# Two-block transformer layer stack: attention scores as pairs of 64-row products, with the gating term in a pass of its own

## The reference

```
for l in range(2):
    h = rms_norm(x, attn_pre_g[l]);  proj = h @ w_in[l]          # 512 x 3080
    qa, ka, va, qb, kb, vb, f_logit = split(proj)                # five 512-wide parts, vb, and 8 forget columns
    # "diff" heads: 4 heads, each with two maps m of 64 features, rotary on qa and ka
    p[m] = softmax(causal(qa[h, m] @ ka[h, m].T / 8))            # m = 0, 1
    oa   = (p[0] - lam * p[1]) @ va[h]                           # va[h] is 128 wide, then rms_norm
    # "fox" heads: 8 heads of 64 features, with a forget gate
    log_f = log_sigmoid(f_logit + forget_bias[l]);  c = cumsum(log_f over tokens)
    ob   = softmax(causal(qb[h] @ kb[h].T / 8 + c[q] - c[k])) @ vb[h]
    x = x + rms_norm(concat(oa, ob) @ w_out[l], attn_post_g[l])
    x = x + rms_norm((silu(h2 @ w_gate[l]) * (h2 @ w_up[l])) @ w_down[l], ffn_post_g[l])
# then the second block: stick-breaking attention, HGRN2 mixer, feed-forward (untouched)
```

## Time and profile before

| | us |
|---|---|
| time, median of 3 runs | 2193.34 |
| profiled execution: time | 2193.14 |
| profiled execution: span | 2191.3 |
| TensorE (PE) busy | 2127.4 |
| VectorE (DVE) busy | 785.8 |
| ScalarE (ACT) busy | 749.4 |
| GpSimd (POOL) busy | 849.6 |

### The profile page before, as it was taken

How to read it: one execution, slowest core, us unless ns; L and a number is a source line. 1 busy time by engine, 2 the same in 40 slices (tenths; PEclk the granted TensorE clock), 3 DMA queues, 4 the chain that set the end, 5 groups by cost and what they waited for, 6 DMA issues and landing times.

```text
span 2191.3 us, 27815 instructions
## 1 busy us (share of the span) xinstructions
PE 2127.4 (97%) x10510; PEld 1759.3 (80%) x10510; DVE 785.8 (36%) x1513; ACT 749.4 (34%) x1287; POOL 849.6 (39%) x390
## 2 busy tenths in 40 slices
PE   8999999999999999999999999998899999999999
PEld 6886798888887876798888887776777789888887
DVE  6327542121004128452111014587566543121200
ACT  4236452222224136452222124444432434222211
POOL 3530134444434430134444434333444344444442
PEclk9999999999999999999999999999999999999999
DMA  5330033333323320033333222211211232333232
GB/s 186 106 96 1 1 92 114 99 98 97 97 87 105 97 77 1 11 97 106 96 96 96 97 86 68 77 49 40 61 45 49 83 110 84 99 96 96 87 101 72
DMA packets 130832, 178.25 MB, mean 81 GB/s; under 512 B 11891, under 2 KB 79790, under 8 KB 130734
## 3 DMA queue, kind: packets, MB, share of 16 engines
q1 hardware_dynamic: 130142, 175.25, 26.2%
q10 hardware_dynamic: 592, 1.64, 0.2%
HBM read 174.76 MB, written 2.10 MB: 81 GB/s over the span
## 4 chain that ended last, share of the span: by engine, by line
PE 39%; issue 32%; POOL 17%; DVE 9%; ACT 3%; POOLq 0%; DMA 0%; ACTq 0%; DVEq 0%
POOL w_lo L571 17%; PE PS L1504 9%; PE PS L1506 9%; PE PS L1505 9%; PE PS L1773 3%; PE PS L1785 2%; PE PS L1906 1%; DVE R L1413 1%; PE PS L1761 1%; DVE R2R L1350 1%; PE PS L1712 1%; DVE R L1421 1%; PE PS L1881 1%; PE PS L1558 1%; PE PS L1873 0%
## 5 line engine op out<-in xcount | busy, mean ns | idle before, releaser
L571 POOL TENSOR_TENSOR w_lo<-R,w_hi 128x1024 fp32r<-128x1024 f32 (+1 forms) x288 | 680.0, 2366 | 950.9 <-ACT w_hi L653 892.5
L653 ACT ACTIVATE w_hi<-R 128x1024 fp32r<-128x1024 f32 (+1 forms) x288 | 299.2, 1042 | 954.0 <-PE PS L1506 953.4
L1504 PE MATMUL PS<-xt_hi,w_hi 128*128 128x512 f32 (+1 forms) x1216 | 458.8, 377 | 0.0
L1506 PE MATMUL PS<-xt_hi,w_lo 128*128 128x512 f32 (+1 forms) x1216 | 453.2, 373 | 0.0
L1505 PE MATMUL PS<-xt_lo,w_hi 128*128 128x512 f32 (+1 forms) x1216 | 453.0, 373 | 0.0
L1504 PE MATMUL PS<-w_hi,xt_hi 128*128 128x512 f32 x928 | 375.5, 405 | 13.1 <-DVE R L1314 6.9
L1506 PE MATMUL PS<-w_hi,xt_lo 128*128 128x512 f32 x928 | 364.2, 392 | 0.0
L1505 PE MATMUL PS<-w_lo,xt_hi 128*128 128x512 f32 x928 | 363.5, 392 | 0.0
L1506 PEld LDWEIGHTS PS<-xt_hi,w_lo 128*128 128x128 f32 x1216 | 229.1, 188 | 40.6
L1505 PEld LDWEIGHTS PS<-xt_lo,w_hi 128*128 128x128 f32 x1216 | 229.3, 189 | 40.4 <-issue 1.0
L1504 PEld LDWEIGHTS PS<-xt_hi,w_hi 128*128 128x128 f32 x1216 | 229.2, 189 | 40.4 <-issue 1.0
(11 more groups left out here) (252 smaller groups left out, 2146.8 us busy)
## 6 DMA issues: line engine op xcount, KB each, us to landing
R<-in_w_in SPq DMA_DIRECT2D x56, 512.0 KB, 3.7
R<-in_w_gate SPq DMA_DIRECT2D x88, 256.0 KB, 2.8
R<-in_w_up SPq DMA_DIRECT2D x88, 256.0 KB, 3.0
R<-in_w_down SPq DMA_DIRECT2D x40, 512.0 KB, 3.8
raw<-in_w_in SPq DMA_DIRECT2D x36, 512.0 KB, 3.7
R<-in_w_out SPq DMA_DIRECT2D x24, 512.0 KB, 3.8
R<-in_w_ffn_gate SPq DMA_DIRECT2D x44, 256.0 KB, 2.8
R<-in_w_ffn_up SPq DMA_DIRECT2D x44, 256.0 KB, 3.0
```

The source lines that it names most:

```text
L571: nc.gpsimd.tensor_tensor(w_lo[:, r, 0:subs, :], raw_of(stage, lap)[:, r, 0:subs, :], w_hi[:, r, 0:subs, :].bitcast(F32), ALU.subtract).th ...
L653: nc.scalar.activation(w_hi[:, r, 0:subs, :], raw_of(stage, lap)[:, r, 0:subs, :], ACT.Copy).then_inc(hi_ready, 1)
L1504: mm(out_, a_hi, b_hi, start=start, stop=False)
L1506: return mm(out_, a_lo, b_hi, start=False, stop=stop)
```

## The change

A pair of units (two maps of a diff head, or two fox heads side by side) is now issued together, at even u. Its two score products have 64 rows each: the first uses partitions 0 to 63 of q and k, the second 64 to 127, and they write two neighbouring banks. The diff q is copied out once, without the zeros. Fox heads are transposed two at a time as full 128-row items, so there are 16 items instead of 24.

The gate is no longer in q and k. Minus c, split into a rounded part and a remainder, is placed by DVE in a tile `decay`, four TensorE transposes (at unit `COLUMNS_AT` = 2) and one ACT copy turn it into `decayT`, and a fox score pair gets a second pair of 64-row products in fp32r with `pair_rows` (0/1 rows that pick the head) over all its columns. Adding c of the query is dropped, since the softmax does not see it. `pair_rows` and the zeroing of `decay` are made by DVE during the projection, after chunk 2.

DVE takes one maximum for the two banks of a pair. The chain that makes c runs beside the transposes, and TensorE computes the sums after the last item. `PRODUCT` goes from 6 to 7 and `OUTPUT` from 7 to 8.

```diff
-JOIN, TURN, PRODUCT, OUTPUT = 2, 5, 6, 7
+JOIN, TURN, PRODUCT, OUTPUT = 2, 5, 7, 8
+COLUMNS_AT, SUMS_BANK, COLUMNS_BANK = 2, 6, 7
...
-            items1 += [(QA[:, :, cols], P, [q[:, h, :] for q in QAT], one_head[:, 0, :]), (KA[:, :, cols], P, KAT[:, h, :], 1.0)]
-        for h in range(8):
-            items1 += [(QB[:, :, h, :], 66, QBT[0:66, h, :], HD ** -0.5), (KB[:, :, h, :], 66, KBT[0:66, h, :], 1.0)]
+            items1 += [(QA[:, :, cols], P, QAT[:, h, :], HD ** -0.5), (KA[:, :, cols], P, KAT[:, h, :], 1.0)]
+        for h in range(4):
+            cols = slice(h * P, (h + 1) * P)
+            items1 += [(QB[:, :, cols], P, QBT[:, h, :], HD ** -0.5), (KB[:, :, cols], P, KBT[:, h, :], 1.0)]
...
-        units1 += [("fox", (h, 0), i) for h in range(8) for i in range(T)]
+        units1 += [("fox", (2 * pair + m, m), i) for pair in range(4) for i in range(T) for m in range(2)]
...
+                        if u == COLUMNS_AT:
+                            act.wait_ge(c_turned, l + 1)
+                            nc.scalar.activation(decayT, PS[:, COLUMNS_BANK, :], ACT.Copy).then_inc(c_copied, 1)
...
+                dve.wait_ge(c_mm, l + 1)
+                c_sum = PS[:, SUMS_BANK, 0:T * 8].rearrange("p (t a m) -> p t a m", a=4, m=2)
+                parts = [decay_r[:, :, HD * m:HD * m + 8].rearrange("p t (a b) -> p t a b", b=2) for m in range(2)]
+                for m in range(2):
+                    ins = V.tensor_scalar(parts[m][:, :, :, 0], c_sum[:, :, :, m], -1.0, None, ALU.mult)
+                link(ins)
+                for m in range(2):
+                    ins = V.scalar_tensor_tensor(parts[m][:, :, :, 1], c_sum[:, :, :, m], -1.0,
+                                                 parts[m][:, :, :, 0].bitcast(F32), ALU.mult, ALU.subtract)
+                ins.then_inc(c_placed, 1)
...
-                        V.tensor_reduce(nmax[:, u % 4:u % 4 + 1], PS[:, u % 4, 0:P * (i + 1)], AX.X, ALU.max,
-                                        negate=True).then_inc(max_done, 1)
+                    if u < len(units1) and u % 2 == 0:
+                        i, bank = units1[u][2], u % 4
+                        dve.wait_ge(s_mm, b + u + 2)
+                        V.tensor_reduce(nmax[:, bank:bank + 2], PS[:, bank:bank + 2, 0:P * (i + 1)], AX.X, ALU.max,
+                                        negate=True).then_inc(max_done, 2)
...
                         if b + u >= 4:
-                            pe.wait_ge(exp_done, b + u - 3)
-                        mm(PS[:, u % 4, 0:upto], q, kk, start=True, stop=False)
-
-                        mm(PS[:, u % 4, upto - P:upto], ident_b[:, :], causal_b[:, :], start=False, stop=True).then_inc(s_mm, 1)
+                            pe.wait_ge(exp_done, b + u - 2)
+                        if kind == "fox":
+                            pe.wait_ge(c_copied, l + 1)
+                        for m in range(2):
+                            mm(PS[:, u % 4 + m, 0:upto], q[halves[m], pair, upto - P:upto], kk[halves[m], pair, 0:upto],
+                               start=True, stop=False)
+                        if kind == "fox":
+                            for m in range(2):
+                                mm(PS[:, u % 4 + m, 0:upto], pair_rows[halves[m], pair, :], decayT[halves[m], 0:upto],
+                                   start=False, stop=False)
+                        for m in range(2):
+                            mm(PS[:, u % 4 + m, upto - P:upto], ident_b[:, :], causal_b[:, :], start=False,
+                               stop=True).then_inc(s_mm, 1)
+                    if u == COLUMNS_AT:
+                        pe.wait_ge(c_placed, l + 1)
+                        for t in range(T):
+                            last = nc.tensor.transpose(PS[:, COLUMNS_BANK, t * P:(t + 1) * P], decay[:, t, :], ident[:, :])
+                        last.then_inc(c_turned, 1)
```

More of the change, by code:

```diff
@@ L260, in build @@
         rot = at2(16560, 4, T, ROT * 8)
-        QBT = at1(0, 8, SEQ)
-        KBT = at1(4096, 8, SEQ)
+        QBT = at1(0, 4, SEQ)
+        KBT = at1(2048, 4, SEQ)
+        decay = at2(18608, T, P)
+        decay_r = at2r(18608, T, P)
+        decayT = at2r(17584, 1, SEQ)[:, 0, :]
+        pair_rows = at2r(18096, 4, P)
         YG_out = at2(4096, T, D).rearrange("p t (k n) -> p t k n", n=P)
@@ L1155, in attention1 @@
                     src = banks(c % 2)
[L1156 to L1163, removed]
+                    if c == 5:
+                        V.tensor_copy(VB[:, :, :, 0:HD], heads(src, 8)).then_inc(evac[1], 1)
+                    elif c >= 2:
+                        V.tensor_copy(dst[c], src).then_inc(evac[c % 2], 1)
+                        if c == 2:
+                            V.memset(VB[:, :, :, HD:HD + 1], 1.0)
+                            V.memset(decay, 0.0)
+                            for n in range(4):
+                                own = ident[:, :].rearrange("p (m r) -> p m r", m=2)[:, :, 2 * n:2 * n + 2]
+                                ins = V.tensor_reduce(rsum[:, n:n + 1], own, AX.XY, ALU.add)
+                            link(ins)
+                            for n in range(4):
+                                ins = V.tensor_scalar(pair_rows[:, n, :], SUMS[:, ONES, :], rsum[:, n:n + 1], None, ALU.mult)
+                            ins.then_inc(pair_rows_done, 1)
                     else:
@@ L1734, in attention1 @@
                     transpose_item(n, base, items1, 2 + n % 6, 6)
-                pe.wait_ge(f_gate, l + 1)
-                mm(PS[:, 0, 0:8 * T], SUMS[:, UPTO, :], fy[:, 2, :, :], start=True, stop=False)
-                for back in range(1, T):
-                    last = mm(PS[:, 0, 8 * back:8 * T], SUMS[:, ONES, :], fy[:, 2, 0:T - back, :],
-                              start=False, stop=back == T - 1)
-                last.then_inc(c_mm, 1)
-                pe.wait_ge(c_placed, l + 1)
                 for n in range(8, len(items1)):
@@ L1746, in attention1 @@
                 pe.wait_ge(tr_dve, (base + len(items1)) // 2)
+                pe.wait_ge(f_gate, l + 1)
+                sums = PS[:, SUMS_BANK, :]
+                mm(sums[:, 0:8 * T], SUMS[:, UPTO, :], fy[:, 2, :, :], start=True, stop=False)
+                for back in range(1, T):
+                    last = mm(sums[:, 8 * back:8 * T], SUMS[:, ONES, :], fy[:, 2, 0:T - back, :],
+                              start=False, stop=back == T - 1)
+                last.then_inc(c_mm, 1)
                 b, bo, bj = len(units1) * l, n_out * l, n_join * l
@@ L1763, in attention1 @@
                         last.then_inc(pt_mm, 1)
[L1764 to L1775 removed]
+                    if u < len(units1) and u % 2 == 0:
+                        kind, (h, _), i = units1[u]
+                        upto = P * (i + 1)
+                        pair, q, kk = (h, QAT, KAT) if kind == "diff" else (h // 2, QBT, KBT)
+                        halves = slice(0, HD), slice(HD, P)
+                        if b + u >= 4:
+                            pe.wait_ge(exp_done, b + u - 2)
+                        if u == 0:
+                            pe.wait_ge(pair_rows_done, l + 1)
+                        if kind == "fox":
[10 more added lines that the diff above has]
+                               stop=True).then_inc(s_mm, 1)
```

59 lines of the change are left out of this document (25 added, 34 removed).

## The result

The changed kernel takes 2174.59 us (median of 4 runs, 2172.83 to 2175.07), the kernel before on the same chip 2193.32 us (2190.09 to 2193.53). The ratio is 0.9917 with an interval of 0.9899 to 0.9934: faster, by 0.8%. The prediction had 2187.7 us in a range of 2174 to 2206, so the sign and the range hold, the range by 0.6 us, and the number is that of rival (a), both maps side by side. The profiled execution took 2175.01 us, its span is 2173.2. One of the five executions of the control in experiment 10 took 5568.07 us at a mean granted clock of 0.437 (it is 0.977 to 0.998 in all others), and the ratios leave it out.

What follows compares the result with a forecast made beforehand. TensorE, busy for 97% of the span, was taken as the bound. Front -7.4, diff loop -5.6 and fox loop +7.4 gave -5.6 us from 2193.14 profiled: 2187.5, or 2187.7 us as median, range 2174 to 2206.

Steps and rivals of the forecast that it cites:

- rival (a): Score pairs: both halves fully side by side, a pair costs two pass times; -17 us, 2176.5 us; chance 0.22.
- prediction's own sign: Diff loop, block 3: four score passes span 1.3 us; another span would mean the forecast is wrong.
- The step that failed: Score pairs: only passes 2 and 3 run together, so a pair takes three pass times; diff head -0.98 us.
- Front: Before the first scores: 32 fewer transposes -3.5, waits for ACT -0.55 and for placing c -0.41; -4.46 us per layer.
- Row changes: Score pairs: leaving 128 rows for 64 and returning costs 0.29 us per pair, 1.16 per diff head.
- Rival (d): Score pairs: dearer row changes, 0.4 us instead of 0.29, 7 us more over 64 pairs, 2194.7 us; chance 0.08.
- Masks: Diff loop: masks side by side save one exposed weight load per pair, -0.22 us per head.
- Diff heads: Diff loop: TensorE work -0.3, gap -6.9, new exponential wait +1.6; -5.6 us over eight heads.
- The gap of 0.92: Diff loop: TensorE's wait for ACT's copy before the product with the values goes with PRODUCT 7; about -6.9 us.
- Fox pairs: Fox loop: scores with gate 4.10 against 4.34 us, row changes +1.16; +0.92 per two heads, +7.4 altogether.
- The start of the loop: Unit 2: four decay transposes 0.44 us, their wait covered, plus 0.35 us delay of the exponential by ACT's copy, per layer.
- The rival "slower": Score passes don't overlap, so the change only adds: +12.8 us, 2206 us; chance 0.16.

Runs made afterwards that it cites:

- experiment 10: Changed kernel with longer lags (transposes 7, product 9, output 10): 2175.38 us, ratio 0.9933; its control, the unaltered changed kernel beside it: 2172.83 us.
- experiment 1: Changed kernel with both products of each pair on the same half, rows 0 to 63: 2235.18 us, ratio 1.021.
- experiment 7: Changed kernel, but a fox pair issues scores and gate of the first head, then of the second: 2174.86 us, ratio 0.9923.
- experiment 2: Kernel before, but each diff score product reads only its 64 nonzero rows, one product at a time, masks between: 2235.53 us, ratio 1.0213.
- experiment 5: Kernel before with only the lags changed, PRODUCT 7 and OUTPUT 8: 2189.96 us, ratio 0.9993.
- experiment 4: Changed kernel with the old lags, PRODUCT 6 and OUTPUT 7: 2207.29 us, ratio 1.0072.
- experiment 9: Kernel before with only diff scores as 64-row pairs, masks behind, and the new lags; front, fox heads and maxima as before: 2185.98 us, ratio 0.9975.
- experiment 3: Changed kernel with one maximum per unit on DVE instead of one per pair: 2175.43 us, ratio 0.9924.
- experiment 8: Changed kernel with ACT instead of DVE scaling the diff heads' outputs: 2175.47 us, ratio 0.9925.

## Why the prediction was right in sign and off in size

The range held, but by 0.6 us, and the control of experiment 10 (2172.83 us) lies below it: that it held is partly luck. By the prediction's own sign, another span of the four passes of block 3 than 1.3 us, the forecast's mechanism was wrong.

| both layers, us | predicted | by the traces |
|---|---|---|
| front | -8.9 | -9.4 |
| diff loop, with the start | -4.0 | -6.4 |
| fox loop and tail | +7.4 | -0.4 |

The predicted -4.0 are -5.6 for the heads and +1.6 for `decay` at the start. Most of the miss, 7.8 of 10.7 us, lies in the fox loop.

**The step that failed** is this one: "the second map's first pass can only begin once the first map's second pass has begun ... a pair takes three pass times". It begins at once, and a pair takes two (183.373 and 183.381 us; experiments 1 and 7). The rule that I named under rival (a), from the Trainium skill, "TensorE: Matmul & The Clock Gate", Part 3, products on different row groups starting about 4 ns apart, was the right one. The traces agree, with 4 to 8 ns in the loops of the changed kernel and 6 to 10 for nearly all pairs in experiment 7, for float32 products of two passes and for their weight loads as well. I gave it 0.22 because passes of before start in order; but none of those were on different rows, so they said nothing on it.

**Front:** -4.46 us predicted, -4.75 and -4.69 measured. The transposes, both waits and the sums are where the prediction put them.

**Row changes:** 0.29 us predicted, 0.30 measured, in the changed kernel and in experiment 2. Rival (d) falls.

**Masks:** -0.22 us per head predicted, nothing measured. Two masks side by side take 0.12 us (188.46 to 188.58), as two single ones of 0.06 did.

**Diff heads:** -0.70 us each predicted, -1.33 measured for the third and fourth of each layer. TensorE's own work: scores 0.43 + 0.64 + 0.85 + 1.06 and four entries of 0.09 are 3.34 us, against 4.34: -1.00 where I had -0.04. The gap of 0.92 went and a wait of 0.55 came, -0.37 where I had -0.66. I had named the chain of maximum and exponential as what comes next, at 0.2 us; what came was DVE's join, which the prediction put at nothing. It stood right behind: experiment 5, the lag alone, gives 1 to 2 us and not the 6.9 of the sum. Lag and pairs need each other: pairs with the old lag lose 1.80 us per head again, and clock beside it (experiment 4), the lag without pairs is worth 1 to 2 us, both are worth 5.6 (experiment 9). I had added terms that are not independent.

**Fox pairs:** +0.92 us per two heads predicted. Measured are -1.06, -0.12 and +0.27 for the first three pairs of layer 1, and -1.06, +0.13 and +0.55 in layer 2, so that the loop with its tail went from 51.61 to 51.14 and from 51.61 to 51.68 us and not up by 3.7. Own work: spans to the mask 0.49 + 0.75 + 1.02 + 1.30 and 0.36 for the entries are 3.92, against 4.34: -0.42. This is the price that the failed step had too high, by 1.34 us a pair. What makes the third pair positive is waiting that I had not foreseen. After block 0 the product stands 0.45 us later than its work asks for (215.88, a wait for DVE's scaling with 0.28 shown), and before the last transposes there are 0.23 more (214.03 to 214.48 for two products that take 0.22 elsewhere). The pairs bunch the work: two outputs follow each other with no scores in between. That this is the cause is read from the trace only; no run tested it.

**The start of the loop:** +0.79 us per layer predicted for `decay`. Four transposes stand there, behind no wait, 0.54 us at full clock (experiment 3's trace, 162.54 to 163.08). Behind ACT's copy the scores of block 3 wait for the exponential, 0.27 us there and 0.50 in the control of experiment 10: 0.8 to 1.0. In the control the second head then waits 1.02 us for the join where later ones wait 0.55, so the start costs some 1.5 us; in the profiled execution half clock adds 0.85 in layer 1.

**The sum:** -5.6 predicted; -16.2 us by the traces, and -18.7 by the medians, of which some 2 lie in untouched code. The executions of the kernel before alone spread from 2190.01 to 2193.59 us. Rival (a) said -17, with DVE as the bound of the diff loop. That is the right size, though DVE's work is not the bound (experiment 8). Its fox loop, +0.2, came out at -0.4, and its diff loop, -8.0 with the start, at -6.4.

**Not in the prediction at all** was the clock. I took it as full from the page, whose slices are 55 us wide; the windows above show half clock in the kernel before too, though none in the attention of that execution. The rival "slower" had only serial passes in it, at 2206 us. Serial passes on 64 rows in fact give 2235 (experiment 1), and the difference is about the 29 us of its lower clock.

## What to carry to other kernels

Two float32 products of 64 rows each are worth placing on the two halves of the array: they take the time of one, weight loads included. Each such group pays 0.30 us for leaving 128 rows and coming back, so leave no 64-row product alone. The gain grows with the columns: with the entry, a pair to its mask takes 1.15 us at 512 columns where four passes took 1.72, and 0.52 at 128 where they took 0.43. When such a step makes scores shorter, the waits that they covered come out: change the lags with it, and price the two as one. Read the clock in windows of a few microseconds and not from a page's slices. Before counting a gap as gain, look for the wait that ends just before it does.

## What the runs showed of the hardware that I had not expected

- Each half of the rows works through its own products: first passes start some 10 ns apart even with three passes of the other half ahead of them in the program (experiment 7).
- Going from 128 to 64 rows costs 0.09 us, going back with the first load 0.21; 0.30 in all, the same for a pair as for a single product.
- With 64-row products one at a time, the granted clock fell to 1.2 GHz in the loops and stayed there for 13.7 and 47.8 us (experiment 1) and 17.1 and 34.1 us (experiment 2), with TensorE busy throughout these stretches though not ahead of them. In the fox loops of experiment 1 the same kind of products also ran at 2.4 GHz. The loops of the kernel before and of the changed one kept 2.4 GHz, but for 3.4 us at the start of a loop in some executions of the changed one. With more idle time (experiment 4) it also fell, in stretches of 3.4 to 13.7 us. What decides it these runs do not settle.
- At half clock DVE and ACT keep their speed (in experiment 1 the maximum of a block 3 pair takes 1.23 us at either clock, its exponential 0.69 and 0.68), so many of the waits for them vanish and TensorE can read as 100% busy, as in the window of 48 us in experiment 1. A stage without gaps is no sign of health; the clock column has to be read beside it.
